# Recurrence of an RWKV block: half of each chunk's scores and turns written to the other half of the partitions, and K times v computed ahead of the chain

## The chip, the cores and the metric

One core of one Trainium2 chip runs the whole program. The metric is the device time of one execution in microseconds: 3371.77 us is the median of 3 runs of the kernel before (3365.54 to 3376.61). Lower is better.

## The reference, cut to what matters

The program is a small stack: an RWKV-7 mixer with a dense feed-forward, a pooling mixer with a mixture of experts, then an attention block with a convolutional feed-forward, on 512 latent and 256 context tokens of width 1024, all in fp32. The change touches only the recurrence of the RWKV-7 mixer, for 16 heads of width 64 and two directions:

```python
def wkv7_scan(s0, r, w, kk, a, k, v):
    def step(s, inp):
        r_t, w_t, kk_t, a_t, k_t, v_t = inp
        s_kk = jnp.einsum('bhvk,bhk->bhv', s, kk_t)
        s = (s * w_t[:, :, None, :] - s_kk[..., None] * (kk_t * a_t)[:, :, None, :]
             + v_t[..., None] * k_t[:, :, None, :])
        return s, jnp.einsum('bhvk,bhk->bhv', s, r_t)
```

The state of the context's scan is where the latent scan starts; the second direction runs on flipped tokens.

## The kernel before, in words

The function `pairs` computes the recurrence. Two heads (a pair) fill the 128 partitions, 64 each (`heads`), so each of the 8 pairs goes through the engines once. The 768 tokens are cut into 12 chunks of 64 (n = 0 to 3 context, 4 to 11 latent); a quad is four chunks, a pair has three quads. Both directions d stand side by side in the free dimension.

For each chunk PE computes, with multiplies of 64 x 64 by 64 columns, one for each head and direction:

- **score** (L1048): B and K against A, and for latent chunks against R as well, into PSUM bank i = n % 4. DVE multiplies them with a mask into `LK` (L1314). POOL adds the identity and makes the first transposed operand (L936, L939), DVE transposes it (`first`, L1318).
- **trans** (L1064): A, K, v and B times the identity, that is their transposes, into bank 4. ACT copies them to `TR` (L1226).
- **X** and **T** (L1072, L1084), five levels: the triangular inverse by doubling. DVE masks X (`xs`, L1324), ACT copies T (`tb`, L1230), DVE transposes it (`turn`, L1321).
- **akv** (L1095, L1098): two products that the chain will need, into bank 5, copied by ACT to `AT` (L1234).
- the chain: **U** (L1107, L1110; ACT copies it negated to `Us`, L1238), **Y** (L1132 to L1136; output of a latent chunk, three products, bank 4; ACT copies it, L1247), **Z** (L1117, L1119; the new state, K times v and B times U). DVE adds the old state (L1330) and multiplies with the decay at the chunk's end (L1335) into `Zb`, which the next U reads.

The order of all engines is written out by hand. `quad(g)` lists a quad: for each i score n of the current quad, akv of the quad before, trans n; then first; then for each level the X of all four chunks and the T of all four, and behind each of these groups one entry of `links`, which holds the chain of the quad before: U, then Y and Z. The transposes of T (`turn`) are strewn between. Between these entries `plan` spreads the feature work of the next pair and the output work of the pair before, in proportion to the number of entries: wide multiplies on PE (L953 and others), activations on ACT, scans and reciprocals on DVE, and on POOL elementwise operations of 512 to 1536 columns (L869 to L894). Every engine walks the same list and does its own entries in order. `Marks` turns the names into semaphore values: `did(x)` counts one up, `at(x, p)` is the value to wait for.

The tiles in question: `LK` and `TR` lie in the weight ring, two sets of four chunks; `AT` holds four chunks; bank 4 of PSUM is shared by all transposes and by Y.

Of the kernel before, what the change touches and what calls it, by code (L numbers as in the profile page):

```python
# [17 lines left out]
ALU = mybir.AluOpType  # L18
# [3 lines left out]
P = 128  # L22
# [289 lines left out]
class Kernel:  # L312
# [341 lines left out]
    def pairs(self, TW, TA, TG, YG, xr, s_wr):  # L654
# [6 lines left out]
        FRONT = ("score", "trans", "first", "X", "T", "turn")  # L661
# [4 lines left out]
        def lat(n):  # L666
            return n >= CCH
# [18 lines left out]
        def quad(g):  # L686
# [61 lines left out]
        pe_f = self.marks("front_pe", [x for x in fronts if x.rstrip("0123456789.") in ("score", "trans", "X", "T")])  # L748
        pe_c = self.marks("chain_pe", links)
        act_f = self.marks("front_act", following(fronts, {"trans": ["tr"], "T": ["t"]}))  # L750
        act_c = self.marks("chain_act", following(links, {"akv": ["akv"], "U": ["U"], "Y": ["Y"]}))
        dve_f = self.marks("front_dve", following(fronts, {"score": ["LK"], "first": ["first"], "X": ["x"], "turn": ["turn"]}))
        dve_c = self.marks("chain_dve", [y for x in links if x[0] == "Z" for y in ([f"sum{x[1:]}"] if x != "Z0" else []) + [f"z{x[1:]}"]])
# [10 lines left out]
        with ExitStack() as st:  # L764
# [11 lines left out]
            TB, AT, Xs = self.sb(st, "tb", 2, 4, 2, 2, CH), self.sb(st, "at", 4, 2, 2, CH), self.sb(st, "xs", 4, 2, CH)  # L776

            LK = ring.all[:, 0:8 * 512].rearrange("p (s i d o n) -> p s i d o n", s=2, i=4, d=2, o=4)
            TR = ring.all[:, 8 * 512:16 * 512].rearrange("p (s i d o n) -> p s i d o n", s=2, i=4, d=2, o=4)
            heads = (slice(0, CH), slice(CH, P))  # L780
            pair0 = COLS["pair"][0]
# [16 lines left out]
            with nc.Block() as block:  # L798
                @block.sync
                def _(sp):  # L800
# [26 lines left out]
                    for p in range(2, N):  # L827
# [3 lines left out]
                        sp.wait_ge(pe_f.sem, pe_f.at(f"trans{NCH - 1}", p - 2))  # L831
# [4 lines left out]
                def _(pool):  # L836
                    def feature(x, p):
# [14 lines left out]
                        if x == "ex0":  # L852
                            pool.wait_ge(f_dve.sem, f_dve.at("scan0.2", p))
                            if p >= 2:
                                pool.wait_ge(pe_f.sem, pe_f.at(f"trans{NCH - 1}", p - 2))
# [40 lines left out]
                    def output(x, p):  # L896
# [5 lines left out]
                        if x == "y":  # L902
                            pool.wait_ge(act_c.sem, act_c.at(f"Y{NCH - 1}", p))
# [13 lines left out]
                    for kind, p, x in plan:  # L917
# [13 lines left out]
                        if head == "score":  # L931
                            if p == 0 and n == 0:
                                pool.wait_ge(s_diag, 2)
                            pool.wait_ge(dve_f.sem, dve_f.at(f"LK{n}", p))
                            M = LK[:, s, i, :, 0, :]
# [7 lines left out]
                def _(pe):  # L943
# [56 lines left out]
                    for kind, p, x in plan:  # L1000
# [31 lines left out]
                        if head == "score":  # L1032
# [5 lines left out]
                            if n >= 4:  # L1038
                                pe.wait_ge(act_f.sem, act_f.at(f"t{LAST}.{n - 4}", p))
                            elif p:  # L1040
                                pe.wait_ge(act_f.sem, act_f.at(f"t{LAST}.{n + 8}", p - 1))
                            for d in range(2):
                                for o, w in ((0, FB), (2, FK)):
                                    for half in range(1 + lat(n)):
                                        for hh in heads:
                                            to = 256 * d + (o + half) * CH
                                            src = FR[hh, d, chunk_at(n, d) - CTX:chunk_at(n, d) - CTX + CH] if half else FA[hh, d, at(d)]
                                            last = pe.matmul(ps[hh, i, to:to + CH], w[hh, d, at(d)], src, start=True, stop=True)  # L1048
                        elif head == "trans":
# [1891 lines left out]
```

## Time and profile before

| | |
|---|---|
| median of 3 runs | 3371.77 us |
| profiled execution, its own time | 3371.36 us |
| its span | 3369.7 us |
| PE busy | 2928.1 us (87%) |
| DVE busy | 1900.6 us (56%) |
| ACT busy | 1347.0 us (40%) |
| POOL busy | 536.5 us (16%) |
| mean granted clock of TensorE | 0.936 |

Busy times are the union of an engine's operations; PE is the multiplies, their weight loads are counted apart and run beside them. The span is from the first to the last instruction of the profiled execution; the remaining 1.7 us of its time lie around it. The recurrence is one stretch of this span, some 775 us long.

### The profile page before, as it was taken

What the parts mean: (1) busy time and instruction counts of PE and PEld (TensorE: products, weight loads), DVE (VectorE), ACT (ScalarE), POOL (GpSimd) and SP (SyncE); (2) the same over time, 40 slices, a digit from 0 to 9 for tenths busy, and PEclk for the clock granted to TensorE, in tenths of its full rate; (3) what the DMA queues carried; (4) which work ended last, traced back from release to release, by engine and by line L of the source; (5) the groups of instructions that cost most, each with busy time, mean ns of one, the idle gap of its engine ahead of it and who ended that gap; (6) DMA issues with size and microseconds to landing.
All of it is one profiled execution on the core that took longest, in us unless ns stands there. A gap on an engine that the chain in (4) does not pass through costs nothing. (4 is left out here: it accounts for less than half of the span.)

```text
span 3369.7 us, 69659 instructions
## 1 busy us (share of the span) xinstructions
PE 2928.1 (87%) x30053; PEld 2329.7 (69%) x30053; DVE 1900.6 (56%) x3045; ACT 1347.0 (40%) x2016; POOL 536.5 (16%) x489
## 2 busy tenths in 40 slices
PE   7998789898999569999456999999939987769999
PEld 3563678878879458887336999999924334548877
DVE  4431565566665246765746888888860035446652
ACT  1002445545454232221225777777720126423331
POOL 3001434545542010000000000000010026200000
PEclk8999999999999689999778999999969979889999
DMA  4543000000000147655109999999812111112222
GB/s 189 215 150 105 19 4 20 20 20 20 20 3 4 75 154 295 262 200 196 66 27 370 371 369 367 364 371 367 318 56 101 57 33 34 50 67 96 94 105 77
DMA packets 73484, 483.06 MB, mean 143 GB/s; under 512 B 11075, under 2 KB 12483, under 8 KB 31728
## 3 DMA queue, kind: packets, MB, share of 16 engines
q1 hardware_dynamic: 58832, 418.48, 33.3%
q0 software_dynamic: 12096, 52.43, 4.1%
q10 hardware_dynamic: 2304, 8.39, 0.6%
q8 instruction: 206, 3.38, 0.4%
q14 instruction: 46, 0.38, 0.0%
HBM read 457.73 MB, written 34.13 MB: 146 GB/s over the span
## 5 line engine op out<-in xcount | busy, mean ns | idle before, releaser
L2156 DVE TENSOR_TENSOR sb_moe_w_lo<-w_ring,sb_moe_w_hi 128x1408 fp32r<-128x1408 f32 (+1 forms) x132 | 255.2, 1934 | 67.8 <-ACT sb_moe_w_hi L2110 67.2
L2056 PE MATMUL ps<-sb_moe_w_hi,sb_x_feat_lo 128*128 128x352 f32 x832 | 274.1, 329 | 11.5 <-DVE sb_moe_w_lo L2156 11.5
L2058 PE MATMUL ps<-sb_moe_w_hi,sb_x_feat_hi 128*128 128x352 f32 x832 | 268.2, 322 | 0.0
L2057 PE MATMUL ps<-sb_moe_w_lo,sb_x_feat_hi 128*128 128x352 f32 x832 | 267.6, 322 | 0.0
L2110 ACT ACTIVATE sb_moe_w_hi<-w_ring 128x2816 fp32r<-128x2816 f32 x80 | 204.2, 2554 | 0.1
L2056 PEld LDWEIGHTS ps<-sb_moe_w_hi,sb_x_feat_lo 128*128 128x128 f32 x832 | 156.8, 189 | 17.3 <-issue 17.3
L2056 PE MATMUL ps<-sb_moe_w_hi,sb_hid_feat_lo 128*128 128x256 f32 x572 | 163.1, 285 | 3.9 <-DVE sb_hid_feat_lo L2182 3.9
L2058 PE MATMUL ps<-sb_moe_w_hi,sb_hid_feat_hi 128*128 128x256 f32 x572 | 161.8, 283 | 0.0
L2057 PE MATMUL ps<-sb_moe_w_lo,sb_hid_feat_hi 128*128 128x256 f32 x572 | 161.8, 283 | 0.0
L231 PE MATMUL ps<-sb_conv_hl,sb_hi_conv 128*128 128x512 f32 x352 | 140.0, 398 | 22.9 <-DVE sb_lo_conv L219 22.9
L231 PE MATMUL ps<-sb_ffn_features,sb_hi_ffn 128*128 128x512 f32 x352 | 140.1, 398 | 22.1 <-DVE sb_lo_ffn L219 22.1
L2057 PEld LDWEIGHTS ps<-sb_moe_w_lo,sb_x_feat_hi 128*128 128x128 f32 x832 | 157.5, 189 | 0.0
L2058 PEld LDWEIGHTS ps<-sb_moe_w_hi,sb_x_feat_hi 128*128 128x128 f32 x832 | 156.8, 188 | 0.0
L1321 DVE STREAM_TRANSPOSE sb_tb<-sb_tb 128x128 f32<-128x128 f32 x384 | 105.8, 298 | 90.3 <-ACT sb_tb L1230 88.2
L1072 PEld LDWEIGHTS ps<-sb_tb,w_ring 64*64 64x64 f32 x3840 | 127.5, 135 | 38.4 <-issue 20.8
L1072 PE MATMUL ps<-sb_tb,w_ring 64*64 64x64 f32 x3840 | 145.5, 220 | 9.6 <-ACT sb_tb L1230 7.4
L1230 ACT ACTIVATE sb_tb<-ps 128x128 f32<-128x128 f32 x480 | 117.4, 278 | 62.8 <-PE ps L1084 59.3
L1314 DVE TENSOR_TENSOR w_ring<-ps,sb_mask_score 128x512 f32<-128x512 f32 (+1 forms) x96 | 57.8, 602 | 148.9 <-PE ps L1048 148.9
L233 PE MATMUL ps<-sb_conv_hh,sb_hi_conv 128*128 128x512 f32 x352 | 140.6, 399 | 0.0
L232 PE MATMUL ps<-sb_conv_hh,sb_lo_conv 128*128 128x512 f32 x352 | 138.8, 394 | 0.0
L233 PE MATMUL ps<-sb_ffn_features,sb_hi_ffn 128*128 128x512 f32 x352 | 138.2, 393 | 0.0
L232 PE MATMUL ps<-sb_ffn_features,sb_lo_ffn 128*128 128x512 f32 x352 | 138.0, 392 | 0.0
(501 smaller groups left out, 7816.7 us busy)
## 6 DMA issues: line engine op xcount, KB each, us to landing
w_ring<-w_moe_up SPq DMA_DIRECT2D x67, 1408.0 KB, 8.3
sb_hm<-w_ada SPq DMA_DIRECT2D x48, 1024.0 KB, 6.9
w_ring<-w_ffn SPq DMA_DIRECT2D x22, 1024.0 KB, 4.8
w_ring<-w_up SPq DMA_DIRECT2D x22, 1024.0 KB, 4.9
sb_t_again<-w_moe_up SPq DMA_DIRECT2D x13, 1408.0 KB, 8.3
sb_hm<-w_moe_up SPq DMA_DIRECT2D x13, 1408.0 KB, 8.3
sb_b_again<-w_moe_up SPq DMA_DIRECT2D x13, 1408.0 KB, 8.0
w_ring<-w_moe_down SPq DMA_DIRECT2D x13, 1408.0 KB, 7.7
```

The lines of the kernel that those rows point to most:

```text
L231: pe.matmul(out, w_hi[:, at:at + P], lo(k), start=(k == 0), stop=False)
L232: pe.matmul(out, w_lo[:, at:at + P], hi(k), start=False, stop=False)
L233: last = pe.matmul(out, w_hi[:, at:at + P], hi(k), start=False, stop=(k == KT - 1))
L1072: last = pe.matmul(ps[hh, i, d * CH:(d + 1) * CH], M[hh, d, 0, :], tb[hh, d, 0, :], start=True, stop=True)
L1230: S.activation(TB[:, s, i, :, int(lev == LAST), :], ps[:, i, 256:384].rearrange("p (d n) -> p d n", d=2), ACT.Copy).then_inc(*act_f.did("t ...
L1314: V.tensor_tensor(LK[:, s, i, :, ::by, :], ps[:, i, :].rearrange("p (d o n) -> p d o n", d=2, o=4)[:, :, ::by, :], mC[:, :, ::by, :], ALU. ...
L1321: V.transpose(TB[:, s, i, :, 1, :], TB[:, s, i, :, 0, :]).then_inc(*dve_f.did(x))
L2056: pe.matmul(out, x_lo, w_hi, start=first, stop=False)
L2057: pe.matmul(out, x_hi, w_lo, start=False, stop=False)
L2058: return pe.matmul(out, x_hi, w_hi, start=False, stop=end)
L2110: S.activation(WH[:, s, :], raw[r], ACT.Copy).then_inc(rounded[s], 1)
L2156: return V.tensor_tensor(WL[:, s, w], raw[raw_at(c, i)[0]][:, w], WH[:, s, w].bitcast(F32), ALU.subtract)
```

## The change

`trans` disappears as an entry; its multiplies follow the scores of the same chunk in one entry. B against A and R, and the transposes of A, K stay in the own half of the partitions (bank i, now with the transposes of the own half in its upper 256 columns). Of each head, K against A and R, and the transposes of the other set, are written to the other head's partitions (bank 4). In detail:

```diff
+            out += [(pp, f"akA{n}") for n in prev]
             for i in range(4):
                 out += [(p, f"score{n}") for n in cur[i:i + 1]]
-                out += [(pp, f"akv{n}") for n in prev[i:i + 1]]
-                out += [(p, f"trans{n}") for n in cur[i:i + 1]]
+                out += [(pp, f"akO{n}") for n in prev[i:i + 1]]
...
-                links += [[(pp, f"U{n}")], [(pp, f"Y{n}")] * lat(n) + [(pp, f"Z{n}")] * (n < NCH - 1)]
+                links += [[(pp, f"U{n}")], [(pp, f"Z{n}")] * (n < NCH - 1) + [(pp, f"Y{n}")] * lat(n)]
...
+            both_ways = tuple(zip(heads, heads[::-1]))
```

PE, the scores with the turns (the waits on bank 4 are now ahead of both):

```diff
                             if n:
-                                pe.wait_ge(act_f.sem, act_f.at(f"tr{n - 1}", p))
+                                pe.wait_ge(act_f.sem, act_f.at(f"trO{n - 1}", p))
+                                pe.wait_ge(dve_f.sem, dve_f.at(f"LKO{n - 1}", p))
...
+                                for half in range(1 + lat(n)):
+                                    to = d * P + half * CH
+                                    for hh, oo in both_ways:
+                                        x_in = FR[hh, d, chunk_at(n, d) - CTX:chunk_at(n, d) - CTX + CH] if half else FA[hh, d, at(d)]
+                                        pe.matmul(ps[hh, i, to:to + CH], FB[hh, d, at(d)], x_in, start=True, stop=True)
+                                    for hh, oo in both_ways:
...
+                                        pe.matmul(ps[oo, 4, to:to + CH], FK[hh, d, at(d)], x_in, start=True, stop=True)
+                                for o, (own, other) in enumerate(((FA[:, d, at(d)], FK[:, d, at(d)]), (FB[:, d, at(d)], v[:, at(d)]))):
+                                    to = 256 + d * P + o * CH
+                                    for hh, oo in both_ways:
+                                        pe.matmul(ps[hh, i, to:to + CH], own[hh], ident[hh, hh], start=True, stop=True)
+                                    for hh, oo in both_ways:
+                                        last = pe.matmul(ps[oo, 4, to:to + CH], other[hh], ident[hh, hh], start=True, stop=True)
```

akv becomes akA (A against the inverse, bank i, ahead of the quad's scores, which wait for its copy) and akO, which reads the other half and writes the own one: two products, and a third for a latent chunk. K times v and the v part of Y are among them, copied to `AT`. Z and Y keep what depends on U:

```diff
+                                for hh, oo in both_ways:
+                                    pe.matmul(ps[hh, 5, to:to + CH], M[oo, 1, d, 0, :], tr[oo, 1, d, 1, :], start=True, stop=True)
+                                for hh, oo in both_ways:
+                                    last = pe.matmul(ps[hh, 5, P + to:P + to + CH], tr[oo, 1, d, 0, :], tr[oo, 1, d, 1, :],
                                                      start=True, stop=True)
+                                if lat(n):
+                                    for hh, oo in both_ways:
+                                        last = pe.matmul(ps[hh, 5, 2 * P + to:2 * P + to + CH], tr[oo, 1, d, 1, :], M[oo, 1, d, 1, :],
+                                                         start=True, stop=True)
...
                         elif head == "Z":
...
-                                    pe.matmul(ps[hh, 5, to:to + CH], tr[hh, d, 1, :], tr[hh, d, 2, :], start=True, stop=False)
-                                for hh in heads:
-                                    last = pe.matmul(ps[hh, 5, to:to + CH], tr[hh, d, 3, :], Us[hh, d, :], start=False, stop=True)
+                                    last = pe.matmul(ps[hh, 5, to:to + CH], tr[hh, 0, d, 1, :], Us[hh, d, :], start=True, stop=True)
```

ACT copies bank 4's transposes (`trO`), waits for DVE's `LKE`, then copies bank i's (`trE`), 256 columns each. It no longer copies Y. On DVE:

```diff
                             dve.wait_ge(pe_f.sem, pe_f.at(x, p))
+                            V.tensor_tensor(LK[:, s, i, 0, :, halves_in, :],
+                                            ps[:, i, 0:256].rearrange("p (d o n) -> p d o n", d=2, o=2)[:, :, halves_in, :],
+                                            mC[:, :, halves_in, :], ALU.mult).then_inc(*dve_f.did(f"LKE{n}"))
+                            dve.wait_ge(act_f.sem, act_f.at(f"trO{n}", p))
+                            V.tensor_tensor(LK[:, s, i, 1, :, halves_in, :],
+                                            ps[:, 4, 0:256].rearrange("p (d o n) -> p d o n", d=2, o=2)[:, :, halves_in, :],
+                                            mC[:, :, halves_in, :], ALU.mult).then_inc(*dve_f.did(f"LKO{n}"))
...
+                        elif head == "U" and n < NCH - 1:
+                            dve.wait_ge(act_c.sem, act_c.at(f"akO{n | 3}", p))
+                            held = AT[:, i, 2]
+                            if n:
+                                dve.wait_ge(dve_c.sem, dve_c.at(f"z{n - 1}", p))
+                                V.tensor_tensor(Zs[:, :, :], held, Zb[:, n % 2, :, :], ALU.add).then_inc(*dve_c.did(f"pre{n}"))
+                                dve.wait_ge(dve_c.sem, dve_c.at(f"pre{n}", p))
+                                held = Zs
+                            for d in range(2):
+                                c = chunk_at(n, d) // CH
+                                last = V.tensor_scalar(Zs[:, d, :], held[:, d, :], PE2[:, u, d, c:c + 1], None, ALU.mult)
+                            last.then_inc(*dve_c.did(f"ends{n}"))
                         elif head == "Z":
...
+                            dve.wait_ge(dve_c.sem, dve_c.at(f"ends{n}", p))
+                            for d in range(2):
+                                c = chunk_at(n, d) // CH
+                                last = V.scalar_tensor_tensor(out=Zb[:, (n + 1) % 2, d, :], in0=ps[:, 5, 3 * P + d * CH:3 * P + (d + 1) * CH],
+                                                              scalar=PE2[:, u, d, c:c + 1], in1=Zs[:, d, :], op0=ALU.mult, op1=ALU.add)
```

Y's last step is a DVE addition of bank 4 and the v part in `AT`. Waits elsewhere that named `trans`, `tr` or ACT's Y name their successors.

## Rows read from the trace of the kernel before

**Rows 1.** Stretches: us, busy time of each engine, clock, DMA share, GB/s.
```profile
345.00:1120.00 775.00, 697.39 (x19462) 624.70 (x19462) 452.38 (x1358) 367.67 (x1001) 332.64 (x309) 0.98 0.05 14
706.00:735.60 29.60, 27.00 (x814) 24.72 (x808) 17.43 (x53) 15.32 (x45) 25.95 (x18) 1.00 0.16 50
735.60:774.80 39.20, 36.04 (x872) 30.30 (x870) 19.78 (x62) 18.37 (x45) 12.34 (x14) 0.96 0.01 3
774.80:803.40 28.60, 25.20 (x763) 23.33 (x764) 21.14 (x60) 13.99 (x38) 6.96 (x10) 1.00 0.01 4
```
**Rows 2.** Timeline, one score step: start us, us, engine, line, operation, shapes, count.
```profile
701.36 0.28 PE L1048 MATMUL ps<-sb_ex,sb_sg 64*64 64x64 f32 x4
...
701.58 0.60 ACT L1226 ACTIVATE w_ring<-ps 128x512 f32<-128x512 f32 x1 [0.47 <-PE ps L1064]
...
702.98 0.38 ACT L1234 ACTIVATE sb_at<-ps 128x256 f32<-128x256 f32 x1 [0.80 <-PE ps L1098]
...
703.70 0.28 PE L1048 MATMUL ps<-sb_ex,sb_sg 64*64 64x64 f32 x4
```
**Rows 3.** Timeline, a wide multiply pair.
```profile
640.09 1.56 PE L953 MATMUL ps<-sb_tw,sb_w_pair 128*128 128x384 f32 x4
```
**Rows 4.** Waits, 347 to 1120 us: total us, times, longest us.
```profile
PE ps L1107 <- DVE sb_Z L1335: 35.9, 32, 2.7
...
PEld ps L1072 <- DVE sb_tb L1318: 8.1, 16, 1.1
```
**Rows 5.** Groups by shape, 347 to 1100 us: busy us, mean ns, idle before.
```profile
L1335 DVE TENSOR_TENSOR sb_Z<-sb_Z_sum,sb_pend 128x128 f32<-128x128 f32 x77 | 56.7, 736 | 2.6
...
L1314 DVE TENSOR_TENSOR w_ring<-ps,sb_mask_score 128x256 f32<-128x256 f32 x32 | 13.6, 424 | 65.1 <-PE ps L1048 65.1
```
**Rows 6.** Lines L1335 and L1324: duration ns, least/median/most.
```profile
L1335 DVE TENSOR_TENSOR sb_Z<-sb_Z_sum,sb_pend x80: 291/293/3169, 395.8 to 1116.1; 128x128 f32<-128x128 f32 x80
...
L1324 DVE TENSOR_TENSOR sb_xs<-ps,sb_mask_level x480: 224/274/293, 355.3 to 1096.5; 128x128 f32<-128x128 f32 x160
```
**Rows 7.** Timeline, one long L1335.
```profile
518.03 3.43 POOL L872 TENSOR_TENSOR sb_ex<-sb_ex,sb_kk 128x1536 f32<-128x1536 f32 x1
518.44 3.16 DVE L1335 TENSOR_TENSOR sb_Z<-sb_Z_sum,sb_pend 128x128 f32<-128x128 f32 x1
...
521.40 3.50 POOL L876 TENSOR_TENSOR sb_sg<-sb_sg,sb_Pi 128x1536 f32<-128x1536 f32 x1
...
521.74 0.33 PE L1107 MATMUL ps<-sb_at,sb_tb 64*64 64x64 f32 x4 [1.55 <-DVE sb_Z L1335]
```
**Rows 8.** Timeline of POOL, 706 to 731 us.
```profile
706.56 3.47 POOL L869 TENSOR_TENSOR sb_sg<-sb_a,sb_kk 128x1536 f32<-128x1536 f32 x1
...
718.24 3.44 POOL L879 TENSOR_TENSOR sb_a<-sb_a,sb_k 128x1536 f32<-128x1536 f32 x1 [1.38 <-ACT sb_a L1170]
721.76 3.44 POOL L882 TENSOR_TENSOR sb_Pi<-sb_a,sb_Pi 128x1536 f32<-128x1536 f32 x1
725.16 2.46 POOL L888 TENSOR_TENSOR sb_FR<-sb_cs,sb_r 128x1024 f32<-128x1024 f32 x1
...
730.16 0.47 POOL L936 TENSOR_TENSOR w_ring<-w_ring,sb_id_twice 128x128 f32<-128x128 f32 x1
```
**Rows 9.** Timeline of PE in attention, two short stretches.
```profile
2790.16 1.09 PE L2548 MATMUL ps<-sb_hm,sb_vv 128*64 128x128 f32 x16
...
2798.98 1.06 PE L2544 MATMUL ps<-sb_hm,sb_vv 128*128 128x128 f32 x8
```
**Rows 10.** Line L1309: duration ns, least/median/most.
```profile
L1309 DVE COPY sb_mask_turned<-sb_mask_level x2: 183/1741/3299, 328.5 to 331.7; 128x64 f32<-128x64 f32 x2
```
**Rows 11.** Timeline of POOL at L1309.
```profile
327.68 4.08 POOL L869 TENSOR_TENSOR sb_sg<-sb_a,sb_kk 128x1536 f32<-128x1536 f32 x1 [32.96 <-DVE sb_kk L1272]
```
**Rows 12.** Groups of DVE over the whole span: busy us, mean ns.
```profile
L1551 DVE TENSOR_SCALAR sb_ada_acc<-sb_hm,sb_c_silu 128x512 f32<-128x512 f32 x24 | 11.6, 484 | 38.1 <-DMA sb_hm<-w_ada 38.1
...
L2629 DVE COPY sb_hm<-ps 128x512 f32<-128x512 f32 x16 | 11.0, 689 | 10.4 <-PE ps L2532 10.4
```

More of the change, by code:

```diff
@@ L660, in pairs @@
         NG, LAST, H6, MASKS = N * QUADS, 4, TOK // 2, 12
-        FRONT = ("score", "trans", "first", "X", "T", "turn")
+        FRONT = ("score", "first", "X", "T", "turn")
         SC_CUTS = ((0, 256), (256, 512), (512, 768))
@@ L746, in following @@
             return [y + x[len(x.rstrip("0123456789.")):] for x in names for y in table.get(x.rstrip("0123456789."), ())]
-        pe_f = self.marks("front_pe", [x for x in fronts if x.rstrip("0123456789.") in ("score", "trans", "X", "T")])
+        pe_f = self.marks("front_pe", [x for x in fronts if x.rstrip("0123456789.") in ("score", "X", "T")])
         pe_c = self.marks("chain_pe", links)
[L750 to L753, printed above, removed]
+        act_f = self.marks("front_act", following(fronts, {"score": ["trO", "trE"], "T": ["t"]}))
+        act_c = self.marks("chain_act", following(links, {"akA": ["akA"], "akO": ["akO"], "U": ["U"]}))
+        dve_f = self.marks("front_dve", following(fronts, {"score": ["LKE", "LKO"], "first": ["first"], "X": ["x"], "turn": ["turn"]}))
+        dve_c = self.marks("chain_dve", [y for x in links if not (x[0] == "U" and x == f"U{NCH - 1}")
+                                         for y in {"U": ["pre", "ends"], "Z": ["z"], "Y": ["Y"]}.get(x[0], ())
+                                         for y in ([y + x[1:]] if (y, x) != ("pre", "U0") else [])])
         pool_f = self.marks("front_pool", following(fronts, {"score": ["I", "firstT"]}))
@@ L1038, in _ @@
                             if n >= 4:
-                                pe.wait_ge(act_f.sem, act_f.at(f"t{LAST}.{n - 4}", p))
+                                pe.wait_ge(act_c.sem, act_c.at(f"akA{n - 4}", p))
                             elif p:
[L1041 to L1044, printed above, removed]
-                                        for hh in heads:
[L1046 to L1049, printed above, removed]
+                                pe.wait_ge(act_c.sem, act_c.at(f"akA{n + 8}", p - 1))
                             if n == 0:
@@ L1084, in _ @@
                                     last = pe.matmul(ps[hh, i, to:to + CH], w, src, start=True, stop=True)
-                        elif head == "akv":
+                        elif head == "akA":
                             pe.wait_ge(act_f.sem, act_f.at(f"t{LAST}.{n}", p))
+                            for d in range(2):
+                                for hh in heads:
+                                    last = pe.matmul(ps[hh, i, d * CH:(d + 1) * CH], tr[hh, 0, d, 0, :], tb[hh, d, 1, :],
+                                                     start=True, stop=True)
+                        elif head == "akO":
+                            pe.wait_ge(dve_f.sem, dve_f.at(f"LKO{n}", p))
@@ L1093, in _ @@
                             for d in range(2):
[L1094 to L1098 removed]
+                                to = d * CH
```

114 lines of the change are left out of this document (53 added, 61 removed).

## Prediction, written before the result was known

> **What bounds the kernel now.** I read the stretches first, then the step order of one score phase, then who waits for whom, then the two engines around the longest wait. The recurrence fills 345 to 1120 us of the span and PE is busy for 697 of its 775 us [rows 1], so PE work is the first bound. Eight pairs of heads run, each in three quads of four chunks; the first X of one quad to that of the next takes 39.2, 28.6 and 29.6 us, 97.4 together [rows 1].
>
> A multiply of one head and direction shows as two records, and a group of four records (both heads) starts every 0.117 us [rows 2], so one multiply costs 58.3 ns while two quarters of the array are in use. Per pair there are 160 score multiplies (8 for each of 4 context chunks, 16 for each of 8 latent ones), 192 turns (16 x 12), 480 for X and T, 96 akv, 92 U, 88 Z and 96 Y: 1204, which is 70 us. Fourteen wide multiplies for the features (two of 384 columns, four records, take 1.56 us [rows 3]; ten of these and four of 512) fill about 10 more. The other 16 us of a pair are waits. The largest is U waiting for the state: 35.9 us in 32 places [rows 4]. Its cause is in the state's last step, L1335: the median is 293 ns, the longest 3169 [rows 6], and the mean of 77 is 736 [rows 5], so 77 x 443 ns = 34 us is time in which it was held. The held ones end with a POOL operation: L1335 starts at 518.44, under L872, and ends at 521.60, 0.14 us behind it; U follows at 521.74 [rows 7]. L1324, with one operand from PSUM, is never held (293 ns at most) [rows 6]. So an operation with two SBUF operands stands behind POOL. POOL's long operations come in trains: three from 706.56 and five from 718.24, back to back, until the next quad's own work at 730.16 [rows 8].
>
> **The change part by part.**
>
> *Scores and turns on four quarters.* 352 multiplies per pair now rotate over four quarters. No row shows all four. The bounds: two quarters only (58.3 ns each, nothing gained) and four independent ones (29.2 ns, 10.3 us per pair). The nearest row is L2548, whose two heads share all 128 rows and differ only in columns: 16 records take 1.09 us, where 8 records of the full width (L2544) take 1.06 [rows 9]. Columns thus run beside each other there as rows do in the recurrence, so I take 29.2 ns and keep 58.3 for the range.
> The Trainium skill, "TensorE: Matmul & The Clock Gate", section "Part 3: Packing small matmuls", says that a weight load overlaps running multiplies only where the row group differs. That speaks against this edit and is rival 3; the L2548 row does not look like it, though its weights are half as wide as its columns are long.
>
> *The turn-around of bank 4.* Before, a chunk's scores stood in its own bank and only the turns in bank 4, with the next scores and akv (1.4 us of PE) between: PE ran through, one latent chunk per 2.33 us (701.36 to 703.70) [rows 2]. Now score n+1 waits for both trO and LKO of chunk n, and LKO waits for trO, so the two copies stand in a row: 0.22 us from where PE could go on to ACT's start (701.36 to 701.58) [rows 2], 0.38 for 256 columns on ACT (L1234) [rows 2], 0.42 for 256 columns on DVE (L1314) [rows 5], and an estimated 0.25 for two hand-overs, 0.14 of it as from L1335's end to U's first multiply [rows 7]: 1.27 us. Behind the waiting score on PE stands everything; before it only akO (0.70 or 0.47 us). A latent step is 32 x 29.2 ns + 1.27 = 2.20 us, against 2.33. The gain of the four quarters is nearly all eaten. A context step is 0.70 + 1.1 = 1.8 against 1.87. Ahead of the scores stand now four akA (0.93 us, PE works), and the last chunk's X comes 2.2 us behind its score (0.27, LKE 0.42, two POOL operations of 0.46, a transpose, hand-overs) with about 1.4 us of PE work over it, where before 2.1 us covered it and PE waited 8.1 us in the 24 quads, 0.33 each [rows 4]. Sum of a latent score phase: 1.03 + 3 x 2.20 + 0.93 + 2.2 = 10.8 against 4 x 2.33 + 0.70 + 0.33 = 10.4: +0.4 us; context: 1.03 + 3 x 1.8 + 0.7 + 2.0 = 9.1 against 8.3: +0.8. If only two quarters run at once, 10.3 us come on top.
>
> *K times v out of Z, and out of Y.* 44 and 32 multiplies leave the link phase: 4.4 us of PE. They go into akO, under the turn-around, so cost nothing. With Z ahead of Y, the state is ready 0.7 us earlier; one DVE step of the chain goes.
>
> *pre, ends and z.* Per link DVE had two operations of 0.29 us [rows 6, 7]. It now has pre (two SBUF operands), two ends of 64 columns (one SBUF operand, one scalar), two z (PSUM), and for a latent chunk Y: about +0.36 us of DVE per link, +0.2 with Y. pre is the kind that was held; it stands one X-to-T group earlier than L1335, and DVE is in order, so turns, z and the next xs are queued behind it and PE waits for z. Cover from pre to the next U is T 0.93, Z 0.23, Y 0.47, X 0.93 = 2.57 us, less what DVE still owes (ends, three turns, z: 1.5): about 1 us of holding is free, where before none was. If pre alone is held, the 5.3 us of U waits in a pair fall to about 2.3.
> Whether ends are held decides the sign. The nearest row: L1309, a copy of 64 columns with one SBUF operand, was held 3299 ns [rows 10], under L869 (from 327.68 for 4.08 us) [rows 11]. A tensor_scalar of 512 columns takes 484 ns where a copy of 512 columns from PSUM takes 689 [rows 12], so it too goes faster than one column per step. I take ends to be held like the copy. Low bound: never held. The worst of it: between pre and ends there is a wait of DVE on itself. When pre gets through at the end of a POOL operation, POOL's next one, already queued (L876 begins at 521.40, while L1335 ends at 521.60) [rows 7], goes ahead of ends, and DVE stands through a second whole operation.
> The Trainium skill, "SBUF — State Buffer", section "Who interferes with whom", states that a tensor_scalar in a two-port mode, and a VectorE instruction with two SBUF inputs, contend with GpSimd, whoever comes first keeping the pair for its whole instruction. For two inputs this trace agrees (3169 ns); for a tensor_scalar beside POOL no row shows it.
>
> **The sum, per pair, by quads.** Third quad (706.0 to 735.6), walked with [rows 8] (the present times of U and of the scores are from the same stretch, not shown): pre of the first link at 707.2 is held until 710.1, ends until 713.5, U at 714.4 (before 713.7). pre held until 717.0, ends fall in the gap before 718.24, U at 718.1 (before 717.3). pre held until 721.8, ends behind L882 until 725.3, U at 726.3 (before 722.0). The last ends stand behind L891. The scores begin 4.4 us later than now (726.8); 1.3 come back, since today the phase lasts 8.8 us for 7.5 us of multiplies because POOL is busy until 730.16 [rows 8], and by then it will be done; the context score phase gives +0.8: +4.0 us. First quad (39.2 us): score phase +0.4, links -1.6, chain -0.3, DVE +0.5: -1.0. Second quad (28.6 us), where DVE is busy 21.1 us, eight reciprocals among it [rows 1]: the 0.9 us saved on PE is hidden behind DVE, which gets 4 x 0.36 more; score phase +0.4, chain -0.3: +1.5. Together +4.5 us per pair, +36 for eight. The profiled execution took 3371.4 us (span 3369.7 and 1.7 around it), 0.4 below the median of the runs, so: 3407 us.
>
> **Rivals.**
> 1. Held ends, four quarters (above): 3407, own range 3385 to 3440. Chance 0.42.
> 2. ends not held. Third quad: U follows at 711.1, 714.5 and 717.9, but POOL's train ends at 730.2 all the same, so the gain is about 1.3 us less the 0.8 of the score phase. With -1.0 and +1.5 of the others: 0.0 us per pair, 3371. For it: no tensor_scalar was seen held. Against: L1309. Chance 0.20.
> 3. No overlap beyond two quarters: 10.3 us per pair on top of rival 1, about 2 to 3 of them hidden by POOL and DVE: +60 us, 3467. For it: no row with four. Against: L2548. Chance 0.13.
> 4. Faster. The score phases lose their waits (ACT or DVE turn bank 4 round faster than single operations show, or akO and features cover it) and holding stays at today's level. Then the first quad gains 2.8 + 1.6 us, the third is bounded by POOL at 1.3, the second by DVE at nothing: -5.7 us per pair, 3326. It decides from a turn-around below about 0.8 us. Chance 0.25.
>
> Two runs of this kernel can be told apart from about 0.3%, 10 us. Faster by more: rival 4 and a third of rival 2, 0.31. Same: 0.10. Slower: 0.59. The range 3330 to 3455 leaves out most of rival 3 and the best of rival 4.
>
> **What would show it.** Right: tensor_scalar rows of 64 columns with medians near 0.2 us and maxima above 3; PE idle before score for DVE's LKO, some 0.5 us each; groups of score records in half of 0.117 us; the state's waits larger in the third quad alone. Wrong: score multiplies still at 58.3 ns (rival 3); ends never above 0.3 us (rival 2); no idle before scores (rival 4). The rest of the kernel, 2595 us of the span, should not move; if it does, the prediction is wrong for a reason not seen here.

## The result, and the profile after

The changed kernel takes 3470.18 us (median of 4 runs, 3464.21 to 3471.39) against 3371.44 for the kernel before beside it (3365.54 to 3376.61): ratio 1.029, 95% interval 1.0269 to 1.0311. The direction was forecast (chance 0.59), the size was not: 99 us slower where 36 were forecast and 84 was the end of the range.

The loss lies in the recurrence, and most of it in the third quad of each pair. Stretches of the kernel after, as in [rows 1]: the whole recurrence, then a third, a first and a second quad, from the first X to the next first X.

```profile
345.00:1210.00 865.00, 661.80 (x19444) 579.21 (x19446) 595.61 (x1777) 393.68 (x1126) 329.19 (x306) 0.93 0.04 13
748.40:791.00 42.60, 28.11 (x806) 25.92 (x807) 33.55 (x75) 16.78 (x50) 26.13 (x18) 0.84 0.11 34
791.00:828.20 37.20, 31.13 (x848) 25.14 (x848) 22.49 (x77) 18.10 (x48) 11.74 (x13) 1.00 0.01 3
716.30:748.40 32.10, 24.13 (x796) 21.34 (x796) 24.08 (x78) 16.40 (x48) 7.24 (x12) 1.00 0.02 5
```

Against 29.6, 39.2 and 28.6 us in [rows 1] the third quad lost 13.0 us (forecast +4.0), the first won 2.0 (forecast -1.0), the second lost 3.5 (forecast +1.5). Nearly all of the 13.0 us stand ahead of the third quad's scores: counted from its first X, the last three U start at 11.7, 17.1 and 27.1 us (forecast 8.4, 12.1 and 20.3; before 7.7, 11.3 and 15.9) and the first score at 33.6 (forecast 25.2; before 20.8). In the third quad VectorE is busy for 33.55 us where it was 17.43, and the granted clock is 0.84 instead of 1.00.

Groups of DVE by shape, 345 to 1212 us (busy us, mean ns, idle before), and the lines of `pre` (L1351) and `ends` (L1356), with least, median and longest ns. They answer to L1335 in [rows 5, 6].

```profile
L1356 DVE TENSOR_SCALAR sb_Z_sum<-sb_Z_sum,sb_pend 128x64 f32<-128x64 f32 x160 | 109.4, 726 | 2.8
L1351 DVE TENSOR_TENSOR sb_Z_sum<-sb_at,sb_Z 128x128 f32<-128x128 f32 x80 | 54.6, 682 | 7.4 <-ACT sb_at L1258 7.4
...
L1351 DVE TENSOR_TENSOR sb_Z_sum<-sb_at,sb_Z x80: 265/282/3060, 395.0 to 1208.3; 128x128 f32<-128x128 f32 x80
...
L1356 DVE TENSOR_SCALAR sb_Z_sum<-sb_Z_sum,sb_pend x160: 242/254/3459, 395.3 to 1208.8; 128x64 f32<-128x64 f32 x160
...
L1363 DVE SCALAR_TENSOR_TENSOR sb_Z<-ps,sb_pend,sb_Z_sum x176: 180/265/285, 392.9 to 1210.0; 128x64 f32<-128x64 f32 x176
```

Mean against median gives the time held: 80 x (682 - 282) ns = 32 us in `pre` and 160 x (726 - 254) ns = 76 us in `ends`, 108 together, where L1335 had 34. L1363, whose first operand is in PSUM, is never held. One link with holds, DVE, POOL and PE:

```profile
749.87 2.37 DVE L1351 TENSOR_TENSOR sb_Z_sum<-sb_at,sb_Z 128x128 f32<-128x128 f32 x1
752.27 6.67 DVE L1356 TENSOR_SCALAR sb_Z_sum<-sb_Z_sum,sb_pend 128x64 f32<-128x64 f32 x2
758.86 0.68 DVE L1341 STREAM_TRANSPOSE sb_tb<-sb_tb 128x128 f32<-128x128 f32 x3
759.48 0.43 DVE L1363 SCALAR_TENSOR_TENSOR sb_Z<-ps,sb_pend,sb_Z_sum 128x64 f32<-128x64 f32 x2
...
748.65 3.44 POOL L872 TENSOR_TENSOR sb_sg<-sb_a,sb_kk 128x1536 f32<-128x1536 f32 x1
752.06 3.46 POOL L875 TENSOR_TENSOR sb_ex<-sb_ex,sb_kk 128x1536 f32<-128x1536 f32 x1
755.48 3.41 POOL L879 TENSOR_TENSOR sb_sg<-sb_sg,sb_Pi 128x1536 f32<-128x1536 f32 x1
...
760.05 0.48 PE L1125 MATMUL ps<-sb_at,sb_tb 64*64 64x64 f32 x4 [6.20 <-DVE sb_Z L1363]
```

`pre` stands to the end of L872 (752.09), the first end to the end of L875, the second to the end of L879: 2 x 64 columns take 6.67 us, one GpSimd operation each. Of the 88 pairs of ends 15 had the first one held, and in 13 of these the second was held again. U then runs at the 1.2 GHz level (the granted clock is 0.50 from 760 to 761 us, behind the 6.2 us in which PE waited for the state): four records in 0.48 us, where L1112 takes 0.28 further below.

Waits of PE after, 345 to 1200 us (us, times, longest), to compare with [rows 4]:

```profile
PE ps L1125 <- DVE sb_Z L1363: 88.0, 29, 7.1
PE ps L1061 <- DVE w_ring L1333: 16.4, 37, 0.9
...
PE ps L1079 <- DVE sb_tb L1338: 12.3, 15, 1.6
...
PE ps L1061 <- ACT sb_at L1253: 10.6, 6, 1.8
PE ps L1061 <- ACT w_ring L1245: 10.0, 24, 0.9
...
PE ps L1070 <- issue: 3.6, 7, 0.7
```

U's wait for the state went from 35.9 to 88.0 us; 26.4 us of waits for bank 4's copies are new (L1333 is LKO; L1245 is trE, which ends within 0.01 us of LKO and steps a counter that the score reads, but by the code the score waits for LKO there too). New as well is a kind of idle time that waits for nothing ("issue"): 21.8 us in 34 places over the recurrence (to 1250 us), against 0.2 us in one place before.

A score phase on four quarters, PE's timeline of a chunk that ends at 707.13:

```profile
706.95 0.23 PE L1068 MATMUL ps<-sb_consts,sb_ex 64*64 64x64 f32 x2
706.96 0.23 PE L1070 MATMUL ps<-sb_consts,sb_Pi 64*64 64x64 f32 x2
707.01 0.23 PE L1068 MATMUL ps<-sb_consts,sb_ex 64*64 64x64 f32 x2
...
707.48 0.28 PE L1112 MATMUL ps<-w_ring 64*64 64x64 f32 x4
708.42 0.27 PE L1061 MATMUL ps<-sb_ex,sb_sg 64*64 64x64 f32 x2 [0.65 <-DVE w_ring L1333]
```

Four records, two multiplies, start every 0.06 us: 29 ns a multiply, as forecast. The next score comes 1.29 us after PE is through with the last turn (at 707.13; forecast 1.27).

Adding up, for the six middle pairs, the time from the start of each PE record to the start of the next, by what the next one is, gives where a pair's time goes (us per pair):

| | before | after | change |
|---|---|---|---|
| scores and turns | 21.1 | 19.4 | -1.7 |
| akv / akA, akO | 5.6 | 11.2 | +5.6 |
| U | 10.8 | 20.2 | +9.3 |
| Z and Y | 11.3 | 8.3 | -3.0 |
| X | 18.7 | 21.9 | +3.2 |
| T | 17.6 | 19.5 | +1.9 |
| features, outputs | 10.9 | 11.3 | +0.4 |
| pair | 96.1 | 111.8 | +15.7 |

The six middle pairs make 94 us of the loss.

### The profile page after: what moved, and what is told of

Same layout as the page of the kernel before. It is cut to its first block and busy times, and to the rows that moved or that the text cites. A ratio compares the mean times of both kernels' runs of the same rounds, so it can differ in the third digit from the quotient of the medians.

```text
span 3467.7 us, 70743 instructions
## 1 busy us (share of the span) xinstructions
PE 2894.1 (83%) x30117; PEld 2287.1 (66%) x30117; DVE 2049.1 (59%) x3469; ACT 1374.1 (40%) x2144; POOL 535.0 (15%) x489
## 3 DMA queue, kind: packets, MB, share of 16 engines
q8 instruction: 207, 3.39, 0.4%
## 5 line engine op out<-in xcount | busy, mean ns | idle before, releaser
L1079 PE MATMUL ps<-sb_tb,w_ring 64*64 64x64 f32 x3840 | 153.8, 228 | 25.4 <-DVE sb_tb L1338 12.3
L1079 PEld LDWEIGHTS ps<-sb_tb,w_ring 64*64 64x64 f32 x3840 | 136.1, 142 | 56.6 <-issue 28.4
L2093 PEld LDWEIGHTS ps<-sb_moe_w_hi,sb_x_feat_lo 128*128 128x128 f32 x832 | 157.0, 189 | 17.1 <-issue 16.7
L1329 DVE TENSOR_TENSOR w_ring<-ps,sb_mask_score 128x256 f32<-128x256 f32 (+1 forms) x96 | 36.5, 380 | 176.8 <-PE ps L1070 176.8
L1262 ACT ACTIVATE sb_Us<-ps 128x128 f32<-128x128 f32 x96 | 26.6, 277 | 276.7 <-PE ps L1128 261.2
```

The lines of the kernel that those rows point to most:

```text
L1079: last = pe.matmul(ps[hh, i, d * CH:(d + 1) * CH], M[hh, 0, d, 0, :], tb[hh, d, 0, :], start=True, stop=True)
L1329: V.tensor_tensor(LK[:, s, i, 0, :, halves_in, :], ps[:, i, 0:256].rearrange("p (d o n) -> p d o n", d=2, o=2)[:, :, halves_in, :], mC[:, ...
L2093: pe.matmul(out, x_lo, w_hi, start=first, stop=False)
```

## The experiments

The theories: H1, holding by GpSimd makes nearly all of the loss. R1, the waits of the score phase do. R2, VectorE simply has more to do. H2, the turn-around of bank 4 eats what four quarters give. From the doubled scores on, H3: PE runs out of instructions. Each ratio is to the kernel before, with its 95% interval; "before" is 3369.5 to 3370.0 us in these comparisons.

**One operation in place of two ends.**

```diff
-                            for d in range(2):
-                                c = chunk_at(n, d) // CH
-                                last = V.tensor_scalar(Zs[:, d, :], held[:, d, :], PE2[:, u, d, c:c + 1], None, ALU.mult)
+                            V.tensor_tensor(Zs[:, :, :], held[:, :, :] if n == 0 else Zs[:, :, :], AP(end.tensor, end.offset, [end.ap[0], (step, 2), (0, CH)]),
+                                            ALU.mult).then_inc(*dve_c.did(f"ends{n}"))
```

> The changed kernel (3470 us) with the two tensor_scalars of 'ends' merged into one tensor_tensor of 128 columns with a broadcast second operand. H1 (holding by GpSimd makes nearly all of the loss, and the second end is held anew): the 31.9 us in which the second end was held go, and with them part of the stretches in which the granted clock fell to half: 3430 us, from 3415 to 3440. R1 (the waits of the score phase make most of the loss): the time of a link hardly matters, 3455 to 3470. R2 (VectorE's load): one operation of 0.25 us fewer for each of 88 links, 3450 to 3465.

3433.6 us (3433.0 to 3434.2), ratio 1.0194 (1.0170 to 1.0217): 36.5 us less than the changed kernel, for one operation fewer. U's wait for the state falls from 88.0 to

```profile
PE ps L1125 <- DVE sb_Z L1363: 63.8, 34, 5.6
```

H1 is right to 4 us; the second end was a hold of its own. R1 and R2 gave 3450 or more. In a third quad that begins at 736.9 us the second U now starts here:

```profile
745.34 0.48 PE L1125 MATMUL ps<-sb_at,sb_tb 64*64 64x64 f32 x4 [2.92 <-DVE sb_Z L1363]
```

That is 8.4 us behind the first X. Over the six third quads from 522 to 1095 us the last three U start 8.4 to 8.8, 12.2 to 14.0 and 20.8 to 21.6 us behind it: close to the forecast's walk, 8.4, 12.1 and 20.3, which let both ends pass together. The first score comes at 27.0 to 29.2 us, still later than the 25.2 of the forecast.

**No held operation at all.** PE adds the old state by an identity multiply in Z's group, ACT scales K times v in place, DVE keeps z alone.

```diff
-                                V.tensor_tensor(Zs[:, :, :], held, Zb[:, n % 2, :, :], ALU.add).then_inc(*dve_c.did(f"pre{n}"))
...
+                                        pe.matmul(ps[hh, 5, to:to + CH], ident[hh, hh], Zb[hh, n % 2, d, :], start=True, stop=False)
...
+                                    last = S.activation(AT[:, i, 2, d, :], AT[:, i, 2, d, :], ACT.Copy, scale=PE2[:, u, d, c:c + 1])
...
-                                                              scalar=PE2[:, u, d, c:c + 1], in1=Zs[:, d, :], op0=ALU.mult, op1=ALU.add)
+                                                              scalar=PE2[:, u, d, c:c + 1], in1=AT[:, i, 2, d, :], op0=ALU.mult, op1=ALU.add)
```

> The changed kernel without any link operation on VectorE that reads only SBUF: TensorE adds the old state into the bank by a multiply with the identity, ScalarE scales K times v in place ahead of time, VectorE's two last operations read PSUM. All of the 108 us of holding go; a part of it was hidden. H1: U waits some 10 us instead of 88.6 and the granted clock stays near 0.99: 3365 us, from 3345 to 3385. R1: the score phase keeps its waits and is most of the loss: 3420 to 3445. R2: VectorE loses pre and ends, 0.75 us a link, 66 us in all, without regard to GpSimd: 3400 to 3420, and the state's waits outside GpSimd's trains shrink as well.

3392.9 us (3390.6 to 3395.5), ratio 1.0071 (1.0047 to 1.0096): 77 of the 99 us are gone, though PE makes 40 identity multiplies more for each pair of heads (2.7 us by the starts of its records). A third quad now, and U's wait:

```profile
820.00:849.10 29.10, 26.27 (x838) 23.74 (x838) 14.36 (x63) 17.79 (x58) 26.11 (x18) 1.00 0.15 51
...
PE ps L1125 <- DVE sb_Z L1361: 11.0, 16, 0.9
```

29.1 us, with GpSimd as busy as before (26.11 us) and the clock back at 1.00. The time lies 8 us above H1's range (3345 to 3385) and 7 below R2's (3400 to 3420), and the edit takes VectorE's operations away together with their holds, so this run alone does not part the two; the next one does. R1 gave 3420 or more. What is left over the kernel before is 23 us.

**GpSimd's five long operations in pieces of 256 columns.**

```diff
+                        def cut(out, x0, x1, op):
+                            for lo in range(0, TOK, P):
+                                last = G.tensor_tensor(out[:, :, lo:lo + P], x0[:, :, lo:lo + P], x1[:, :, lo:lo + P], op)
```

> The changed kernel with five of GpSimd's operations of 128x1536 cut into six of 128x256 each, so that one lasts about 0.7 us instead of 4. H1: the longest hold of pre or an end falls from 3.5 us to about 1, unless the pieces in a row keep the port; 56 held operations cost 30 to 40 us instead of 108: 3400 us, from 3385 to 3430 with GpSimd's own train up to 5 % longer. If the pieces keep the port from one to the next, the holds stay at 2 to 3.5 us and the time at 3460 to 3480. R1: 3450 to 3470.

3398.3 us (3394.2 to 3405.5), ratio 1.0096 (1.0071 to 1.0122). H1 gave 3400, R1 3450 or more. VectorE's operations are all there, so R2 falls: 72 us come back by GpSimd's lengths alone, and H1 holds as to what made most of the loss. `ends` in this kernel, and POOL's pieces (five in 3.46 us, 0.69 each):

```profile
L1361 DVE TENSOR_SCALAR sb_Z_sum<-sb_Z_sum,sb_pend x160: 248/254/772, 398.7 to 1140.2; 128x64 f32<-128x64 f32 x160
...
739.34 3.46 POOL L852 TENSOR_TENSOR sb_Pi<-sb_a,sb_Pi 128x256 f32<-128x256 f32 x5
```

The longest end is 772 ns, the longest `pre` 847 ns: a VectorE operation gets in at the border between two GpSimd operations, even in a train without a gap.

**The kernel before without its held operation.**

```diff
-                                V.tensor_tensor(Zs[:, :, :], b, Zb[:, n % 2, :, :], ALU.add).then_inc(*dve_c.did(f"sum{n}"))
...
+                                    last = S.activation(Zs[:, d, :], Zb[:, n % 2, d, :], ACT.Copy, scale=PE2[:, p % 2, d, c:c + 1])
...
+                                    last = V.scalar_tensor_tensor(out=Zb[:, (n + 1) % 2, d, :], in0=b[:, d, :], scalar=PE2[:, u, d, c:c + 1],
+                                                                  in1=Zs[:, d, :], op0=ALU.mult, op1=ALU.add)
```

> The kernel before (3371 us) with the old state times its decay on ScalarE, so that VectorE's state step is two operations with a PSUM operand in place of the held L1335. H1: the 34 us of holding go, some of it was waited for by nobody since GpSimd's train sets the end of the third quad: 3350 us, from 3335 to 3362. Rival: ScalarE's two operations come late or GpSimd's train binds all: 3362 to 3375.

3349.6 us (3344.0 to 3351.5), ratio 0.9943 (0.9923 to 0.9962). That is what H1 had (3350). Holding had cost the kernel before 20 us. With no holding on either side the change costs 3392.9 - 3349.6 = 43 us; that is what H1 does not explain, and the identity multiplies are part of it. The next batches look for it, all on the unheld kernels except where said.

**Two quarters only** (all multiplies that stay on their half first, then those that leave).

```diff
+                            for away in range(2):
+                                for d in range(2):
...
+                                            pe.matmul(ps[oo, 4, to:to + CH] if away else ps[hh, i, to:to + CH], (FK if away else FB)[hh, d, at(d)],
```

> The kernel without held link operations (3393 us), its scores and turns in another order: all multiplies that stay on their own half first, then all that leave on the other half, so that no more than two quarters of the array run at once. The bank and the copies are as before. H2 (four quarters save what was forecast, and the waits before the next score eat it): the 352 multiplies of a pair go back from 29.2 to 58.3 ns with the waits behind them unchanged, +10.3 us a pair: 3470 us, from 3450 to 3480. Rival (ScalarE, VectorE or GpSimd bind the score phase and TensorE's time there is worth little): 3400 to 3430.

3425.8 us (3423.3 to 3433.7), ratio 1.0162 (1.0134 to 1.0191): +33 us, where H2 wanted +77 and its rival +7 to +37. Four quarters are worth 33 us, well under the 82 of 352 x 29.1 ns x 8. H2 falls as stated. The time is in the range of the rival, which had ScalarE, VectorE or GpSimd bind the score phase; but the "issue" waits fall too, from 21.6 to 5.5 us, and the next run bears on which of the two it is.

**Spread banks** (the halves that leave stand in banks 4, 3, 4, 1 for the four chunks).

```diff
+        OTHER = (4, 3, 4, 1)
...
-                                        pe.matmul(ps[oo, 4, to:to + CH], FK[hh, d, at(d)], x_in, start=True, stop=True)
+                                        pe.matmul(ps[oo, OTHER[i], to:to + CH], FK[hh, d, at(d)], x_in, start=True, stop=True)
...
-                            if n:
-                                pe.wait_ge(act_f.sem, act_f.at(f"trO{n - 1}", p))
+                            if n >= 2:
+                                pe.wait_ge(act_f.sem, act_f.at(f"trO{n - 2}", p))
```

> The kernel without held link operations (3393 us), with the halves that leave on the other partitions in banks 4, 3, 4 and 1 for the four chunks of a quad in place of bank 4 for all, so that a score waits for the copies of the chunk two back. H2: the waits of a score for the copies of the chunk before (26.8 us by the waits, some 9 us a pair by the starts of the multiplies, of which the akA copy keeps 1.5) go: 3345 us, from 3325 to 3365. Rival (ScalarE and VectorE have the same copies to make, and the last X waits for them instead): 3375 to 3395.

3376.2 us (10 runs, 3371.4 to 3386.4), ratio 1.0021 (1.0007 to 1.0036): 17 us, not 48. The number is the rival's (3375 to 3395), its reason is not: the last X was to wait instead, but X takes 21.2 us a pair where it took 20.9. The waits for bank 4 are gone, but PE's time in scores and turns stays at 17.2 us a pair (19.5 without the edit; 10.3 would be the multiplies). PE's waits in this kernel:

```profile
PE ps L1076 <- issue: 13.8, 13, 1.5
...
PE ps L1078 <- issue: 7.7, 9, 1.5
PE ps L1123 <- issue: 7.1, 8, 1.3
PE ps L1149 <- issue: 6.4, 3, 2.9
```

All "issue" waits together are 50.2 us in 51 places, against 21.6 in 30 in the kernel it was made from: about what the waits for bank 4 had been (26.8 us). They stand in the middle of a group, with nothing to wait for:

```profile
739.40 0.28 PE L1072 MATMUL ps<-sb_ex,sb_Pi 64*64 64x64 f32 x4
740.83 0.28 PE L1076 MATMUL ps<-sb_consts,sb_ex 64*64 64x64 f32 x2 [1.15 <-issue]
```

Counting the records of PE and its weight loads from the first one as 0, the last one ahead of a gap is number 192 modulo 256 in 50 of the 51 gaps, and in all 34 of the kernel after. A DMA queue that brings instructions moves packets of 16384 bytes (207 of them are 3.39 MB in the kernel after), and it is PE's: over the recurrence of that kernel 156 packets land for 39912 records, 256 each. Of 47 such gaps in the kernel with spread banks 42 end 1.4 us, within 0.15 us, behind the landing of one. In the kernels run here the shortest time between two such landings is 3.1 to 3.4 us. A 64x64 multiply takes four instructions (two MATMUL and two LDWEIGHTS records), so 256 instructions are 64 multiplies: 3.7 us on two quarters at 58.3 ns, 1.9 us on four. That is H3: on two quarters the supply just keeps up, on four it does not.

**The same banks in the changed kernel itself** (the same edit as the last one).

> The same edit of the banks, made on the changed kernel itself (3470 us), whose held operations stay. H1 and H2 together: 26 us of waits before a score go, a part is given back in longer waits for GpSimd's train: 3445 us, from 3430 to 3460. Rival R1 (the score phase makes most of the loss): under 3420.

3459.8 us (3458.9 to 3469.4), ratio 1.0265 (1.0236 to 1.0294): 10 us, at the slow end of the range (3430 to 3460). Its "issue" waits rise from 21.8 to 44.6 us. R1, which gave under 3420, is out.

**More cover for the turn-around** (two akA and the first two X0 between the scores).

```diff
-            out += [(pp, f"akA{n}") for n in prev]
+            out += [(pp, f"akA{n}") for n in prev[:2]]
...
+                out += [(pp, f"akA{n}") for n in prev[i + 2:i + 3]]
+                out += [(p, f"first{n}") for n in cur[i - 2:i - 1] if i > 1]
+                out += [(p, f"X0.{n}") for n in cur[i - 2:i - 1] if i > 1]
```

> The kernel without held link operations (3393 us), with only two of the four akA ahead of the scores, the other two and the first two X0 between the scores, as cover for the turn-around of bank 4. H2: up to 0.93 us a quad goes under the waits: 3375 us, from 3365 to 3388. Rival (ScalarE's copy of akA between trE and the next trO makes the turn-around longer): 3393 to 3410.

3417.0 us (3411.2 to 3420.7), ratio 1.0140 (1.0108 to 1.0172): 24 us slower than its base and beyond both forecasts (H2 3375, its rival 3393 to 3410). The X0 stand ahead of scores in PE's order and wait for their transpose, and the scores behind them wait too (11.1 us in 13 in the base):

```profile
PE ps L1083 <- DVE sb_tb L1352: 45.3, 63, 1.5
```

**Each score and turn twice** (spread banks; the repeats write the same values to the same place).

```diff
-                            for d in range(2):
+                            for d in (0, 1, 0, 1):
```

> The kernel without held operations and with the spread banks (3376 us), in which each score and turn multiply is made twice with the same operands into the same place. New theory H3: TensorE's instructions come in blocks of 256 (its gaps without a wait all stand at the same place of such a block: 49 gaps, 53 us), a new block every 3.4 us at the fastest in any run so far, and a multiply of 64x64 takes four instructions; so 352 multiplies more in each of 8 pairs are 5.5 blocks a pair, 18.7 us: +120 to +150 us, 3500 to 3525, with 3 times as many gaps at that place of the block. Rival H2 (four quarters run at 29.2 ns a multiply for as long as wanted): +10.3 us a pair, 3440 to 3462.

3539.3 us (3533.1 to 3542.8), ratio 1.0501 (1.0481 to 1.0520): +163 us, twice H2's +82 and 14 above H3's range. One pitch of 29.1 ns for 2816 multiplies is 82 us; "issue" waits rise by 62, from 50.2 to 111.7 us; the other 19 I have not traced.

```profile
PE ps L1076 <- issue: 29.1, 24, 2.0
PE ps L1078 <- issue: 28.5, 20, 1.9
...
PE ps L1069 <- issue: 15.9, 15, 1.7
PE ps L1072 <- issue: 15.1, 14, 1.6
```

**Fewer instructions for the same columns** (spread banks; the two scores of a latent chunk with the same weights are one multiply of 128 columns; for that the two moving operands stand in one tile).

```diff
-                                for half in range(1 + lat(n)):
-                                    to = d * P + half * CH
...
+                                        if lat(n):
+                                            x_in = AP(x_in.tensor, x_in.offset, [x_in.ap[0], (TOK - CTX, 2), (1, CH)])
+                                        pe.matmul(ps[oo, OTHER[i], to:to + (1 + lat(n)) * CH] if away else ps[hh, i, to:to + (1 + lat(n)) * CH],
+                                                  (FK if away else FB)[hh, d, at(d)], x_in, start=True, stop=True)
```

> The kernel without held operations and with the spread banks (3376 us); the two scores of a latent chunk that share their weights are one multiply of 128 columns in place of two of 64: the same columns through the array, 64 multiplies and 256 instructions a pair fewer, a quarter of those in a latent score phase. H3 (supply of instructions): a third of the 61 us of gaps without a wait go: 3358 us, from 3345 to 3368. Rival H2: the columns are the same, 3372 to 3380.

3358.5 us (10 runs, 3352.7 to 3366.2), ratio 0.9967 (0.9956 to 0.9978): 18 us faster, where H3 said 18 and H2 none. "Issue" waits fall from 50.2 to 23.4 us. Not all of the 18 need be supply: the same edit on two quarters, next, gives 7 us where there is hardly a supply wait to save.

**The same in the kernel before without its hold, and with Z ahead of Y as well.**

> The kernel before without held link operation (3350 us) with the same scores of 128 columns. H3: with two quarters a block of 256 instructions is used up in 3.6 us, hardly faster than the 3.4 us in which one comes, so nothing is gained: 3345 to 3352. Rival (each multiply of 64 columns has an overhead that a wide one shares): 64 x 30 ns x 8 = 15 us faster, 3330 to 3340.

3343.0 us (3340.0 to 3347.3), ratio 0.9923 (0.9906 to 0.9940): 7 us under its base, 2 beyond the range of H3's "nothing" and short of the rival's 15. "Issue" waits are 4.9 us, 4.5 in the base, so these 7 us have another cause, which stays open.

```diff
-                links += [[(pp, f"U{n}")], [(pp, f"Y{n}")] * lat(n) + [(pp, f"Z{n}")] * (n < NCH - 1)]
+                links += [[(pp, f"U{n}")], [(pp, f"Z{n}")] * (n < NCH - 1) + [(pp, f"Y{n}")] * lat(n)]
```

> The same with Z ahead of Y in the link (the one part of the change that costs nothing), a candidate to beat both kernels: the state is ready 0.7 us earlier in 8 links a pair, and U still waited 12 us for the state without it: 3340 us, from 3330 to 3350. Rival (GpSimd's train or the score phases bind): 3347 to 3352.

3344.6 us (3340.2 to 3348.6), ratio 0.9921 (0.9906 to 0.9935): the order of Z and Y does nothing by itself. These two beat both kernels; against the changed one it is 127 us, against the kernel before 27.

## Why the prediction was right in direction and wrong in size

- Four quarters at 29.2 ns, turn-around of 1.27 us: right, both to 2%.
- `pre` held, `ends` held: right. **The step that failed is the price of `ends` in the walk through the third quad** ("ends until 713.5", "DVE stands through a second whole operation"). In the kernel after it stands through a third: `ends` is two instructions, and the second is held anew 13 times of 15. The walk let both pass together, and [rows 10, 11] show just that: the first of two copies of 64 columns was held 3299 ns under L869, the second took 183 ns, although L872 had begun 0.01 us before it (331.71, 331.72), as L879 had before the second end above (755.48, 755.49). Why the one got through and the other did not is open. POOL's row, kernel before:

```profile
331.71 3.48 POOL L872 TENSOR_TENSOR sb_ex<-sb_ex,sb_kk 128x1536 f32<-128x1536 f32 x1
```

- With one instruction in place of the two ends the walk comes out, and 36.5 us come back, against a miss of 63 (99 - 36).
- The whole miss, as a sum: by the unheld kernels holding costs 77 us in the kernel after and 20 in the kernel before, so the change adds 57; without holding on either side it costs 43. The forecast had 3.1 us a pair for holding in the third quad (scores 4.4 later, 1.3 back), 25 in all, and 11 for everything else. So about half of the miss of 63 us is holding and half the other terms, the score phases above all. The identity multiplies of the unheld kernel stand in the 43, so the first share may be larger and the second smaller.
- "1.3 come back": nothing did. In the third quad shown, the stretch from the first score to the next quad's X takes 9.0 us, before 8.8.
- "The 5.3 us of U waits in a pair" is 4.5 by [rows 4] (35.9 over eight pairs); the sum does not use it.
- The Trainium skill, "SBUF — State Buffer", section "Who interferes with whom", has a tensor_scalar able to contend with GpSimd. For that this case has a row now, and it agrees: 3459 ns in L1356.
- The clock was no term of the sum. Behind the long holds it fell: 0.84 in the third quad shown, and T in the third quads takes 7.3 us a pair by the starts of its records where it took 5.0. In the unheld kernel it is 5.1. So the low clock comes and goes with the holds here; it was not tested apart from them.
- Score phases: forecast +1.6 us a pair. Scores, turns and ak together are +3.9, and X, which holds the wait for the last chunk, +3.2. Two things were missing. K times v "under the turn-around, so cost nothing": akA and akO take 5.6 us a pair more than akv did, where Z and Y lost 3.0, and the turn-around of 1.29 us still shows behind them. And the four-quarter bursts run PE out of instructions: 21.8 us of "issue" in the kernel after, which the place in the block of 256 and the doubled scores show to be supply. The forecast had no term for that; in the kernel before there was 0.2 us of it to see.
- akA ahead of the scores ("0.93 us, PE works") put ACT's features in the way, which was not forecast: PE waited 10.6 us in six places for L1253, held up behind a table load on ACT in the kernel after:

```profile
736.11 1.28 ACT L1205 ACT_TABLE_LOAD   x1
737.41 0.84 ACT L1205 ACTIVATE sb_ex<-sb_ex 128x768 f32<-128x768 f32 x1
738.15 0.76 ACT L1253 ACTIVATE sb_at<-ps 128x128 f32<-128x128 f32 x4
```

- Rival 3 gave 3467, near the measured time, for a reason that is not there: the quarters do overlap. The Trainium skill, "TensorE: Matmul & The Clock Gate", section "Part 3: Packing small matmuls", has weight loads overlap only across row groups; here the two column halves of the same rows, added to the two row halves, bring the pitch of a multiply from 58 to 29 ns, so the measurement decides. A near time is no proof of a mechanism.
- The loss is the recurrence's, as forecast: the last quad's first X is at 1078.1 us before and 1181.2 after, 103 us later, against 99 for the whole.

What stays open: with holding gone on both sides and wide scores in both, the four-quarter layout is still 16 us slower (3358.5 against 3343.0). It carries the identity multiplies, some 21 us of PE by the starts of records, which the other does not; whether it would win without them was not tried. The parts also overlap (spread banks save 17 us unheld, 10 held), so they are no exact split of the 99 us.

## What to carry to other kernels

Count instructions, not steps, when VectorE adds two SBUF operands or runs a tensor_scalar on one beside GpSimd: each can be held to the end of the GpSimd operation then running, so keep the operations of a chain on a PSUM operand, or GpSimd's operations short. Before making small multiplies faster, look at how many instructions a microsecond they will ask for; a gap marked "issue" in the middle of a group is PE waiting for its own program. And when work is moved under a wait, check that the wait is still idle once the other edits are made.

## What the runs showed of the hardware

- **Instruction supply.** PE's instructions come in packets of 16384 bytes, 256 instructions, at best one in 3.1 to 3.4 us, so some 13 ns an instruction; a burst faster than that goes on for a while, then stops for up to 2.9 us (L1149 with spread banks). "Issue" waits in the recurrence: 0.2 us before, 4.5 before without the hold, 5.5 with two quarters, 21.8 after, 50.2 with spread banks, 111.7 with doubled scores, 23.4 with wide ones. The Trainium skill, "Runtime: NRT & Kernel Launch", section "Instruction fetch mechanics", has the blocks of 256, as here, but has their fetch hidden because the sequencer dispatches more slowly; for 64x64 multiplies on four quarters that is not so.
- **Four quarters.** With row half and column half both alternating, 64x64 f32 multiplies start every 29 ns, with two quarters every 58.
- **Holding** ends at the border of GpSimd's operation, even if the next follows at once: 847 ns at most with pieces of 0.69 us, 3459 ns with whole operations. Not every VectorE operation on SBUF is held: the 480 transposes of the kernel after, which read and write SBUF alone (L1338, L1341), take 314 ns at most, its 42 reciprocals (L1284) 953 ns at most with a median of 932.
